# The first microseconds of a two-block kernel in another order: token split, squares and norm sum, weight halves, masks, forget product

## The reference

```python
h = concatenate([meta, x], axis=1)                    # 16 + 256 tokens
h = h * rsqrt(mean(h * h, axis=-1) + 1e-6) * norm_g
proj = einsum('bld,dn->bln', h, w_in)
u_pool, z_pool, q, k, v, z_attn, f_logit, g_pool, g_attn = split(proj, ...)
log_f = log_sigmoid(f_logit + b_forget)               # 8 heads
c = cumsum(log_f, axis=1)
s = einsum('bqhd,bkhd->bhqk', q, k) / 8 + c[q] - c[k] # causal, then softmax and times v
```

## Time and profile before

| | us |
|---|---|
| median of 3 runs | 1259.41 |
| lowest, highest | 1259.34, 1259.95 |
| span of the profiled execution, first to last instruction | 1254.4 |
| PE busy in it | 1224.1 |
| DVE busy | 871.6 |
| ACT busy | 689.3 |

### The profile page before, as it was taken

How to read it: one execution, slowest core, us unless ns; L and a number is a source line. 1 busy time by engine, 2 the same in 40 slices (tenths; PEclk the granted TensorE clock), 3 DMA queues, 4 the chain that set the end, 5 groups by cost and what they waited for, 6 DMA issues and landing times.

```text
span 1254.4 us, 25775 instructions
## 1 busy us (share of the span) xinstructions
PE 1224.1 (98%) x9976; PEld 1201.7 (96%) x9976; DVE 871.6 (69%) x1430; ACT 689.3 (55%) x1027; POOL 97.2 (8%) x106
## 2 busy tenths in 40 slices
PE   7999999999999998999999999999999999999996
PEld 6899999999999998979999999999999989999996
DVE  7576688866665888567766756866665777766653
ACT  7455466665544677456656545644444556544431
POOL 7261000000000014400000000000000010000000
PEclk9999999999999999999999999999999999999998
DMA  8544544554653444113555643554663423555621
GB/s 342 180 136 169 176 168 170 207 197 173 231 201 140 148 177 149 37 35 135 178 191 182 249 173 109 195 199 170 221 226 132 144 84 123 188 193 188 256 93 33
DMA packets 48983, 210.01 MB, mean 167 GB/s; under 512 B 3446, under 2 KB 6020, under 8 KB 44436
## 3 DMA queue, kind: packets, MB, share of 16 engines
q1 hardware_dynamic: 47424, 204.42, 45.7%
q10 hardware_dynamic: 1492, 4.68, 1.0%
HBM read 207.99 MB, written 1.10 MB: 167 GB/s over the span
## 4 chain that ended last, share of the span: by engine, by line
PE 92%; DVE 5%; issue 1%; DMA 1%; ACT 1%; ACTq 0%; DVEq 0%
PE main L1870 27%; PE main L1872 27%; PE main L1871 27%; DVE w_lo L989 1%; PE side L1965 1%; DVE cy L1386 1%; PE main L2299 1%; PE side L1939 1%; PE main L2174 1%; PE side L2174 1%; PE main L2481 1%; PE main L2485 1%; PE main L2483 1%; DMA spread<-delta_rows 0%; PE side L1976 0%
## 5 line engine op out<-in xcount | busy, mean ns | idle before, releaser
L521 ACT ACTIVATE w_hi<-raw 128x1024 fp32r<-128x1024 f32 (+2 forms) x364 | 404.5, 1113 | 309.9 <-PE main L1872 303.4
L1870 PE MATMUL main<-xg_hi,w_hi 128*128 128x256 f32 (+1 forms) x2000 | 567.4, 284 | 1.2 <-DVE w_lo L989 0.8
L1871 PE MATMUL main<-xg_hi,w_lo 128*128 128x256 f32 (+1 forms) x2000 | 564.3, 282 | 0.0
L1872 PE MATMUL main<-xg_lo,w_hi 128*128 128x256 f32 (+1 forms) x2000 | 563.8, 282 | 0.0
L989 DVE TENSOR_TENSOR w_lo<-raw,w_hi 128x1024 fp32r<-128x1024 f32 (+2 forms) x364 | 468.2, 1294 | 7.0 <-ACT w_hi L521 6.2
L1870 PEld LDWEIGHTS main<-xg_hi,w_hi 128*128 128x128 f32 x2000 | 378.6, 189 | 3.0 <-DVE w_lo L989 1.2
L1872 PEld LDWEIGHTS main<-xg_lo,w_hi 128*128 128x128 f32 x2000 | 379.5, 190 | 0.0
L1871 PEld LDWEIGHTS main<-xg_hi,w_lo 128*128 128x128 f32 x2000 | 376.6, 188 | 0.5
L1872 PE MATMUL main<-h_lo,w_hi 128*128 128x256 f32 x704 | 198.5, 282 | 0.0
L1870 PE MATMUL main<-h_hi,w_hi 128*128 128x256 f32 x704 | 198.5, 282 | 0.0
L1871 PE MATMUL main<-h_hi,w_lo 128*128 128x256 f32 x704 | 198.5, 282 | 0.0
(11 more groups left out here) (425 smaller groups left out, 1422.9 us busy)
## 6 DMA issues: line engine op xcount, KB each, us to landing
raw<-in_w_gu_a SPq DMA_DIRECT2D x44, 1024.0 KB, 5.2
raw<-in_w_gu_b SPq DMA_DIRECT2D x44, 1024.0 KB, 5.2
raw<-in_w_down_a SPq DMA_DIRECT2D x16, 1408.0 KB, 5.9
raw<-in_w_down_b SPq DMA_DIRECT2D x16, 1408.0 KB, 6.0
raw<-in_w_in SPq DMA_DIRECT2D x20, 1024.0 KB, 5.3
raw<-in_w_in_a SPq DMA_DIRECT2D x13, 1024.0 KB, 5.2
raw<-in_w_up SPq DMA_DIRECT2D x4, 1024.0 KB, 5.1
raw<-in_w_out SPq DMA_DIRECT2D x4, 1024.0 KB, 5.2
```

Source lines behind the costliest of these rows:

```text
L521: act.activation(w_hi[:, u % RING, 0:n], raw[:, s % RAW, u % 2, 0:n], ACT.Copy).then_inc(hi_ready, 1)
L1870: pe.matmul(dst, a_hi, b_hi, start=first, stop=False)
L1871: pe.matmul(dst, a_lo, b_hi, start=False, stop=False)
L1872: return pe.matmul(dst, a_hi, b_lo, start=False, stop=last)
```

## The change

The change concerns the program's first 24 us.

- SP loads `x0` in four quarters, the first slab as two halves with semaphores of their own (`first_in` for unit 0, `landed[0]` for unit 1), and it issues the masks behind the four slabs, ahead of `x`. ACT no longer issues the masks.
- ACT runs a one-column Sqrt at once, which brings its table load ahead of all chunks. It then splits all 8 chunks without squares, splits unit 0 in two halves (`half_hi`, `hi_ready`) and unit 1, and only then squares, with unit 2 in between after chunk 4; unit 3 and the root follow.
- DVE makes all `xg_lo`, then `w_lo` of unit 0 in two halves (`half_lo`, `lo_ready`) and of unit 1, then the eight adds, then `w_lo` of unit 2, and then `rstd`, `lf` and its loop.
- PE puts the forget product into side bank 2 and no longer waits for `const_in` there; unit 0 waits for its weights by halves; the norm sum stands behind unit 1, and takes over the wait for `const_in`. Unit 3 uses main bank 0 without waiting for an evacuation.

```diff
--- before.py
+++ after.py
@@ -331,7 +331,8 @@
         evac = sem("evac")
         par_in, x_in, mem_in, pos_in, wf_in, wba_in, const_in, mask_in = (
             sem(n) for n in ("par_in", "x_in", "mem_in", "pos_in", "wf_in", "wba_in", "const_in", "mask_in"))
-        x0_in = [sem("x0_in0"), sem("x0_in1")]
+        x0_in = [sem(f"x0_in{j}") for j in range(4)]
+        first_in, half_hi, half_lo = sem("first_in"), sem("half_hi"), sem("half_lo")
         sq_ready, acc_clear, acc_done = sem("sq_ready"), sem("acc_clear"), sem("acc_done")
         xh_ready, xg_ready = sem("xh_ready"), sem("xg_ready")
         qsq_ready, q_summed, q_var, q_scaled, cleared, pair_done, rope_cos = (
@@ -481,11 +482,14 @@
                     load(s0 + j)
-            for j in range(2):
-                half = slice(KC // 2 * j, KC // 2 * (j + 1))
-                sp.dma_start(x0[:, half, :], dram["x0"][:, half, :]).then_inc(x0_in[j], 16)
-            for j in range(RAW):
+            for j in range(4):
+                part = slice(KC // 4 * j, KC // 4 * (j + 1))
+                sp.dma_start(x0[:, part, :], dram["x0"][:, part, :]).then_inc(x0_in[j], 16)
+            sp.dma_start(raw[:, 0, 0, 0:KC * P], dram["w_in1"][0][:, 0, :]).then_inc(first_in, 16)
+            sp.dma_start(raw[:, 0, 1, 0:KC * P], dram["w_in1"][0][:, 1, :]).then_inc(landed[0], 16)
+            for j in range(1, RAW):
                 load(j)
+            sp.dma_start(const[:, K_ROT:], dram["const"][:, K_ROT:]).then_inc(mask_in, 16)
             sp.dma_start(x[:, :, :], dram["x"]).then_inc(x_in, 16)
             for name, n, _ in STREAM:
                 load_all(name, n, RAW if name == "w_in1" else 0)
@@ -570,23 +574,31 @@
             act.dma_start(wf[:, :], dram["w_forget"]).then_inc(wf_in, 16)
             act.dma_start(const[:, 0:K_ROT], dram["const"][:, 0:K_ROT]).then_inc(const_in, 16)
             act.dma_start(pos[:, :], dram["pos"]).then_inc(pos_in, 16)
-            act.dma_start(const[:, K_ROT:], dram["const"][:, K_ROT:]).then_inc(mask_in, 16)
+            act.wait_ge(consts_set, 2)
+            act.activation(root[:, 0:1], one_c, ACT.Sqrt, bias=eps_c)
             act.wait_ge(par_in, 16)
             for k in range(KC):
-                act.wait_ge(x0_in[k // (KC // 2)], 16)
-                square_free(k)
+                act.wait_ge(x0_in[k // (KC // 4)], 16)
                 scale_hi(xg_hi[:, k, :], x0[:, k, :], gain("in1", k))
-                square(x0[:, k, :], TOK, k)
                 if k == 0:
                     act.wait_ge(wf_in, 16)
                     act.activation(wf_hi[:, :], wf[:, :], ACT.Copy).then_inc(small_hi, 1)
-            for u in range(RING):
-                if u == 2:
-                    act.wait_ge(consts_set, 2)
-                    root_of("in1", TOK)
-                split_hi(u)
+            act.wait_ge(first_in, 16)
+            for i in range(2):
+                half = slice(i * KC * P // 2, (i + 1) * KC * P // 2)
+                ins = act.activation(w_hi[:, 0, half], raw[:, 0, 0, half], ACT.Copy)
+                ins.then_inc(hi_ready if i else half_hi, 1)
+            act.wait_ge(landed[0], 16)
+            split_hi(1)
+            for k in range(KC):
+                square_free(k)
+                square(x0[:, k, :], TOK, k)
+                if k == KC // 2:
+                    split_hi(2)
+            split_hi(3)
+            root_of("in1", TOK)
             t0 = FIRST_TILE["in1"]
@@ -1085,22 +1097,26 @@
             begin_norm("in1")
             dve.wait_ge(par_in, 16)
             for k in range(KC):
-                dve.wait_ge(x0_in[k // (KC // 2)], 16)
+                dve.wait_ge(x0_in[k // (KC // 4)], 16)
                 scale_lo(xg_lo[:, k, :], x0[:, k, :], gain("in1", k), xg_hi[:, k, :], k)
-                add(TOK, k)
                 if k == 0:
                     dve.wait_ge(small_hi, 1)
                     low(wf_lo[:, :], wf[:, :], wf_hi[:, :]).then_inc(small_lo, 1)
-            for u in range(2):
-                split_lo(u)
+            for i in range(2):
+                half = slice(i * KC * P // 2, (i + 1) * KC * P // 2)
+                dve.wait_ge(hi_ready if i else half_hi, 1)
+                low(w_lo[:, 0, half], raw[:, 0, 0, half], w_hi[:, 0, half]).then_inc(lo_ready if i else half_lo, 1)
+            split_lo(1)
+            for k in range(KC):
+                add(TOK, k)
+            split_lo(2)
             make_rstd("in1", rstd, TOK)
             t0 = FIRST_TILE["in1"]
             dve.wait_ge(extra_done, 1)
-            dve.tensor_tensor(lf[:, :], main[0][0:8, 0:TOK], rstd[0:8, 0:TOK], ALU.mult).then_inc(evac, 1)
+            dve.tensor_tensor(lf[:, :], side[2][0:8, 0:TOK], rstd[0:8, 0:TOK], ALU.mult).then_inc(evac, 1)
             dve.wait_ge(evac, 1)
             dve.tensor_scalar(lf[:, :], lf[:, :], par[0:8, C_BF:C_BF + 1], None, ALU.add).then_inc(f_ready, 1)
-            split_lo(2)
             def taken(dst, t, scale, rows=P, c=0):
@@ -1998,8 +2014,7 @@
                 ins.then_inc(meta_done, 1)
-            pe.wait_ge(const_in, 16)
-            bank = bank_of(0)
+            bank = side[2]
             pe.wait_ge(small_lo, 1)
             for k in range(KC):
                 pe.wait_ge(xg_ready, k + 1)
@@ -2007,7 +2022,6 @@
                 ins = triple(bank[:, 0:TOK], wf_hi[:, w], wf_lo[:, w], xg_hi[:, k, :], xg_lo[:, k, :],
                              k == 0, k == KC - 1)
             ins.then_inc(extra_done, 1)
-            norm_sum("in1", TOK)
             t0 = FIRST_TILE["in1"]
@@ -2033,10 +2047,21 @@
                                          piece(w_hi, u, 4 * kk, 4), piece(w_lo, u, 4 * kk, 4),
                                          k == 0, k == KC - 1)
                     unit_end(ins)
+                elif u == 0:
+                    pe.wait_ge(half_lo, 1)
+                    for k in range(KC):
+                        if k == KC // 2:
+                            unit_begin(0)
+                        ins = triple(main[t0 % 4][:, 0:SEQ], piece(w_hi, 0, k), piece(w_lo, 0, k),
+                                     xg_hi[:, k, META:TOK], xg_lo[:, k, META:TOK], k == 0, k == KC - 1)
+                    unit_end(ins)
                 else:
                     first = 0 if 4 <= u < 8 or 16 <= u < 20 else META
-                    bank = bank_of(t0 + (u if u < 8 else u - 1))
+                    bank = main[0] if u == 3 else bank_of(t0 + (u if u < 8 else u - 1))
                     project(u, bank[:, 0:TOK - first], xg_hi[:, :, first:TOK], xg_lo[:, :, first:TOK])
+                if u == 1:
+                    pe.wait_ge(const_in, 16)
+                    norm_sum("in1", TOK)
                 if u == 4:
                     pe.wait_ge(rstd_ready, 1)
```

## The result

The changed kernel takes 1261.40 us (median of 19 runs, 1259.13 to 1263.42) against 1259.44 of the kernel before in the same rounds (19 runs, 1256.49 to 1261.10): ratio 1.0016, 95% interval 1.0010 to 1.0022. That is 2.0 us more, 0.16%, with an interval that stays above 1, and 0.1 us above the top of the range on record. The forecast was 1259.6. So the mechanism has to be read against 2.0 us, and the profile says where they may be.

The account below looks back on a forecast made before the run. TensorE, busy 98% of the span, was taken as the bound, with unit 3's start the number to beat: 23.86 against 23.84 leaves span 1254.4; plus 5.0 to the median and 0.2 for uncertain terms, 1259.6 us, range 1257.8 to 1261.3.

Parts of the forecast that it names:

- 6.25 was the term: Forget product's start on PE, once wf_hi, wf_lo and a hand-over follow the forget weights' landing: 6.25, 2.06 earlier.
- The central claim: Start to unit 3: 3.3 us gained at unit 0, but the later norm sum leaves unit 3 at 23.86 against 23.84.
- gain kept: Unit 3: DVE's chain doesn't hold it, PE starts it at 21.15, 2.7 earlier; 1256.7 us, chance 0.05.
- So PE sets it: Norm sum behind unit 1: adds are done at 17.0, PE at 17.65, so PE decides and the sum ends at 18.3.
- the term for unit 0's weights: First slab's first half: 2.1 MB at 412 GB/s take 5.1 us, to 7.4, and with 0.9 it lands at 8.3.
- all before PE asks: DVE's weights: unit 0's halves by 10.0 and 10.6, unit 1 by 12.2, each before PE needs it.
- the row of adds: Sum of squares on DVE: from 12.1, 0.53 per chunk, eight chunks and a wait for unit 2's split, ending near 17.0.
- Unit 2 follows at once: PE behind the norm sum: unit 2 starts at 18.3 without a wait, 2.7 us earlier than the 20.95 of before.
- The bounds: End of the adds: 16.0 if they run back to back, 18.4 at 0.63 each, 17.0 taken.
- Late start (rival 1): Forget weights land at 6.5 as before, every step 1.1 later: 1260.6 us, with slow adds 1261.3; chance 0.14.
- The clock (rival 2): PE's new 2.7 us gap at 21.15 brings a 6.8 us half-clock stretch costing 3.4: 1263.0 us; chance 0.09.
- The median above the span: Whole program: the median of runs stands 5.0 us above the profiled span of 1254.4, for both kernels.

Follow-up runs that it names:

- e2: The changed kernel with squares and adds back between the chunks' splits and the norm sum ahead of unit 0 (e2_inline): 1255.30 us, 0.9961 against before.
- e8: The kernel before with only the new order of squares, adds, root and norm sum; loads, masks and constants as before: 1263.76 us, ratio 1.0041.
- after_again: The changed kernel timed and profiled a second time, no edit: 1261.31 us, ratio 1.0016 to before.
- e9: The kernel before plus early table load, later masks, no constants wait at the forget product, x0 in quarters; unit 0 in one piece: 1257.85 us, ratio 0.9989.
- e5: The changed kernel without POOL's work on the rotary angles, so its result isn't the reference's: 1260.49 us, ratio 1.0007 to before.
- e1_lo3_first: The changed kernel with DVE making unit 3's w_lo ahead of the reciprocal: 1260.89 us, ratio 1.0010 to before.
- before_again: The kernel before, unchanged, timed as if it were a change and profiled a second time: 1260.12 us, ratio 1.0008.
- e11: The changed kernel with the masks back on ACT's queue: 1262.94 us, ratio 1.0029 to before.
- e3: The kernel before plus early table load, masks behind the slabs, constants wait at the norm sum; x0 in halves: 1259.48 us, ratio 1.0003.

## Why the prediction was wrong

**What held.** PE's first wait went where it was expected, behind `wf_lo`, and the product started at 5.74 (6.25 was the term). Unit 0 came at 11.79 (11.95). Unit 0 was right by luck: the fast pace came at 9.05 and not near 12, the forget product was done by 10.8, and PE then waited 1.03 for a late `w_lo`. The central claim, that what is gained at unit 0 is lost again before unit 3 because the new order puts the norm sum behind two units, is what e2 and e8 show. Root to the end of unit 3's `w_lo` is 5.68 us (20.09 to 25.77), forecast 5.46, and 5.25 in after_again; DVE has no hole between reciprocal and that `w_lo`, as said. The rival "gain kept" is out.

**Which step failed.** The sentence "So PE sets it", on the norm sum. It was to start at 17.65, when PE is through with units 0 and 1, with the adds done at 17.0. PE was done at 17.7 and stood 1.63 for the adds, which ended at 19.21; in after_again it stood 1.70. So DVE sets the norm sum, and the late adds add to what the new order of PE gives away.

What made the adds late is the term for unit 0's weights: "at 412 GB/s that is 5.1 us ... 8.3". The first half of the slab landed at 10.3 in one profile and 9.3 in the other, 1.0 to 2.0 late. The 2.1 MB were through at 8.6 in both instead of 7.4, which is the rate; and from there to the landing it took 1.7 and 0.7, where 0.9 was set. The rate is that of a slab in one piece: 412 was read from before, and by e9 against e2_inline the halves bring it to some 300. ACT would have been at its chunks until 8.7 anyway, so 1.6 of the 2.0 come through to it, and 1.7 to DVE: unit 1's `w_lo` ends at 13.92 (12.2), the adds start at 13.83 (12.1). The sentence "all before PE asks" failed with it.

**The second mis-sized term** is the row of adds: 5.38 us from first to last end (13.83 to 19.21), forecast 4.9. In it are 0.56 of POOL's work beside DVE (e5) and a hole of 0.67 while ACT makes unit 2's `w_hi`; the forecast had a wait of that kind in it, without a size. The two buffers of the squares, which the sum counts, have one more effect: ACT made two at 12.56, stood 1.20 us until DVE came to the first add, and could not work ahead.

Adding up for the first profile: norm sum at 19.36 instead of 17.65 is 1.71, the root's start 20.09 instead of 18.35 is 1.74, and 0.22 more lie in the stretch behind it, because unit 2's `w_lo`, which was counted as done before the reciprocal, held the reciprocal until 20.81. 23.86 + 1.96 = 25.82. I had written that the forecast was wrong if the norm sum waited for the adds by over 0.5; it waited 1.6 and 1.7 in the two profiles. "Unit 2 follows at once" failed too: its `w_lo` stands behind all adds on DVE, and PE waited 0.88 for it.

**The bounds were the real error.** I had set 16.0 to 18.4 around the end of the adds, from their durations alone; it was 19.21. The start of the adds carried no range at all. It rested on a rate of half a microsecond of trace. That half microsecond was typical of before, and the error was to carry it over to a kernel with other loads in that stretch. With 2.0 us on the landing, 1.6 of them at the adds, the recorded steps give 18.6 for the last add and 24.8 for unit 3, 1.0 later than forecast; with the slow adds they give 20.0 and 26.2, and the range would have reached 1261.8.

**Late start (rival 1).** Its time, 1260.6 to 1261.3, comes near the result, but not its reason: the forget weights landed early, at 4.9. The chain was late at its other source, the slab.

**The clock (rival 2).** Partly real. The gap was split into three (1.6, 0.9, 1.8) and a half-clock stretch followed in one profile and overlapped in the other, priced 1.6 and near nothing. I had given it 0.09, as an all or nothing case at 3.4; it is a share of executions at some 1.6 or less. How much of the 2.0 between the medians it is, two profiles don't tell. The Trainium skill, page "TensorE: Matmul & The Clock Gate", section "HAM oscillation — how this bites in real kernels", tells of a kernel whose array falls to half clock in each wait for data, with waits longer than any here. The traces agree with the tendency in four of six profiles with these gaps, and not for each wait: e1_lo3_first has a wait of 1.7 for the adds and one of 1.4 at unit 4, and no such stretch in its first 60 us.

**The median above the span.** I carried over 5.0 us as what lies around the span. It is 1.8 in the run of the changed kernel and 2.2 in that of before_again. The rest was that the profiled execution had few half-clock stretches. It cancels in the forecast, which takes the same 5.0 for both kernels, but it hid how wide single executions spread.

**What stays open.** Why two half slabs move at some 300 GB/s where a whole one moves at over 400; that they do is shown. The share of executions in which the new gaps bring a half-clock stretch. How e2's gain over e9 is shared between the halves and the earlier rise of the clock, and the loss between the adds' place and the norm sum's. And a change without the halves, which wasn't made. Last, all seven kernels with the late order lose another 0.3 to 0.7 us between 450 and 484, at a `w_lo` near 473; the others don't, and the reason wasn't looked for.

## What to carry to other kernels

Before starting a bound engine earlier, find the longest serial chain that ends at one of its later units and ask whether the new order moves that chain's first link back; if it does, the gain is handed over at the first unit that needs the chain, and lateness at its source (here a slab's landing) goes most of the way to the end (in e11 1.2 to 2.2 us at the landing, 1.6 in the median). Put a range on the start of such a chain first, not only on the durations in it, and don't take a transfer's rate from a kernel whose loads are cut otherwise. Keep cheap links of the chain (here 0.4 us squares and adds) in the holes between other work: done inline they cost PE 0.7 to 1.5 us at unit 0 and gave back 3.4 to 4.7 at unit 3.

## What the runs showed of the hardware

- Small loads on one queue wait for the rows of a large load on the other: with rows of 4352 bytes `par` and `wf` needed 4.3 and 5.3 us to land, with 2176 bytes 3.2 and 3.6 (e3 and e9, nothing else changed).
- In the changed kernel the 16 DMA engines moved 284 GB/s from 5.7 to 8.8 us at a busy share of 1.00, and 418 from 9.2 to 10.6 at 1.03. Being busy doesn't mean being at full rate. The first window, columns as above:

```profile
5.70:8.80 3.10, 3.06 (x13) 3.06 (x14) 2.15 (x5) 2.18 (x7) 0.07 (x1) 1.00 1.00 284
```

- The pace of 272 columns is 0.227 us at the 1.2 GHz level and 0.127 at 2.4. It changed at 9.1, 9.8, 10.4, 15.3 and 17.1 us in profiles whose PE began at 5.7, 1.3, 5.9, 5.9 and 7.4, and at 14.0 and 12.8 in the two profiles of before, which began at 8.3 and 8.2. So the first matmul's time doesn't tell when. The granted-clock column shows 1.00 in these slow starts as well (the window above): there only the starts of the matmuls tell.
- One slab of 1 MB loaded as two halves of 512 KB goes with a lower rate of all 16 engines: 283 to 329 GB/s from 6 to 9 us in eight profiles, against 401 to 425 in five with one load.
- Half-clock stretches of 3.4 us, or several in a row (6.8, 13.7), appear in one and the same program in changing places while PE counts as busy, and one of 3.4 us near 160 costs 1.5 to 1.7; between 559 and 569 us all 14 profiles have one that begins there.
